# Attended rows stored from ScalarE's queue, four jobs later, in place of SyncE's queue

## The reference

```
z = rmsnorm(x) @ w_in                       # q, k, v and forget gate of group A; q, k, v of group B
A: softmax(q k' / 8 + C[t] - C[s]) v        # 8 heads of 64, causal, C = cumsum(log sigmoid(forget))
B: softmax(q k' / 8 + table[h, t - s]) v    # 8 heads of 64, own chunk of 64 and 8 chunks back
mix = concat(rmsnorm(A), rmsnorm(B)) @ w_out
x = x + rmsnorm(mix);  x = x + rmsnorm(swiglu(rmsnorm(x)))
```

## Time and profile before

| | |
|---|---|
| median of 3 runs | 3012.16 us (3006.19 to 3015.57) |
| profiled execution, its own time | 3007.07 us |
| its span, first to last instruction | 3005.3 us |
| PE busy, of the span | 2845.9 us, 95% |
| DVE, ACT, POOL busy | 57%, 38%, 25% |
| mean granted PE clock | 0.983 |
| `attend`, stretch 640 to 1290 | 650 us, 144 jobs |

### The profile page before, as it was taken

One profiled execution on the slowest core, in us unless ns is written; L12 is line 12 of the kernel. 1 busy time (PEld: TensorE's weight loads), 2 busy tenths in 40 slices (PEclk: granted clock), 3 DMA queues, 4 the chain that ended last, 5 costly groups with the idle time before them and its releaser, 6 DMA issues.

```text
span 3005.3 us, 54881 instructions
## 1 busy us (share of the span) xinstructions
PE 2845.9 (95%) x22143; PEld 2552.1 (85%) x22143; DVE 1709.5 (57%) x3122; ACT 1139.9 (38%) x1904; POOL 754.4 (25%) x683
## 2 busy tenths in 40 slices
PE   7999999979999789969989999999999999999998
PEld 7999999957777567758879999999999997887887
DVE  6222121168788577857788667776766662224443
ACT  5330000046666456645553334333433342223221
POOL 0000000054445123023345434544344420000000
PEclk9999999979999999989999999999999999999999
DMA  5322212152112897467733332332232345335553
GB/s 170 97 71 80 73 62 76 48 168 77 54 49 57 267 297 235 149 203 219 239 111 139 101 108 95 135 114 95 96 113 97 129 140 146 97 96 161 166 167 121
DMA packets 285539, 384.75 MB, mean 128 GB/s; under 512 B 24472, under 2 KB 211112, under 8 KB 273512
## 3 DMA queue, kind: packets, MB, share of 16 engines
q1 hardware_dynamic: 284984, 379.68, 40.0%
q10 hardware_dynamic: 304, 1.57, 0.2%
HBM read 291.91 MB, written 89.28 MB: 127 GB/s over the span
## 4 chain that ended last, share of the span: by engine, by line
PE 44%; issue 6%; DVE 3%; POOL 2%; DMA 1%; ACT 1%; SPq 0%; POOLq 0%; DVEq 0%; ACTq 0%
PE ffn_w L2174 3%; PE ffn_x L2174 3%; PE ffn_w L2177 3%; PE ffn_x L2177 3%; PE ffn_w L2176 3%; PE ffn_x L2176 3%; PE ffn_z L2177 3%; PE ffn_z L2174 3%; PE ffn_z L2176 3%; PE ffn_z L2208 1%; PE ffn_w L2208 1%; PE ffn_y L2174 1%; PE ffn_w L2210 1%; PE ffn_z L2210 1%; PE ffn_y L2177 1%
## 5 line engine op out<-in xcount | busy, mean ns | idle before, releaser
L1214 ACT ACTIVATE att_sx<-att_sx,att_nm 128x640 f32<-128x640 f32 (+17 forms) x272 | 263.4, 971 | 7.4 <-DVE att_nm L1348 7.4
L1225 ACT ACTIVATE att_pts<-att_pt 128x384 f32<-128x384 f32 (+3 forms) x296 | 145.3, 491 | 251.3 <-PE att_pt L1109 236.6
L80 PE MATMUL frt_pz<-frt_xhi,frt_hi 128*128 128x448 f32 (+1 forms) x640 | 230.5, 360 | 0.0
L82 PE MATMUL frt_pz<-frt_xhi,frt_lo 128*128 128x448 f32 (+1 forms) x640 | 230.5, 360 | 0.0
L81 PE MATMUL frt_pz<-frt_xlo,frt_hi 128*128 128x448 f32 (+1 forms) x640 | 230.0, 359 | 0.0
L1109 PEld LDWEIGHTS att_pt<-att_eye,att_sx 64*128 64x128 f32 x3296 | 129.9, 140 | 115.7 <-ACT att_pts L1225 60.1
L515 DVE TENSOR_TENSOR frt_shared<-frt_pz,frt_rb 128x448 f32<-128x448 f32 (+1 forms) x80 | 48.9, 612 | 313.5 <-PE frt_pz L82 313.5
L1109 PE MATMUL att_pt<-att_eye,att_sx 64*128 64x64 f32 x3296 | 166.5, 232 | 55.2 <-ACT att_pts L1225 18.3
L1147 PE MATMUL att_po<-att_pts,att_vv 128*64 128x128 f32 x3296 | 217.2, 279 | 0.3 <-issue 0.3
L1147 PEld LDWEIGHTS att_po<-att_pts,att_vv 128*64 128x64 f32 x3296 | 177.8, 137 | 45.1 <-ACT att_pts L1225 22.7
L1359 DVE COPY att_pts<-att_pt 128x384 f32<-128x384 f32 (+3 forms) x296 | 164.3, 555 | 64.6 <-PE att_pt L1109 58.4
(11 more groups left out here) (327 smaller groups left out, 8300.6 us busy)
## 6 DMA issues: line engine op xcount, KB each, us to landing
ahead_first<-mid_act SPq DMA_DIRECT2D x68, 704.0 KB, 6.7
ahead_second<-in_w_gu SPq DMA_DIRECT2D x33, 1024.0 KB, 5.4
ffn_wr<-in_w_gu SPq DMA_DIRECT2D x33, 1024.0 KB, 5.3
att_raw<-out_zT SPq DMA_DIRECT2D x64, 256.0 KB, 4.7
att_bb<-in_cache_ak SPq DMA_DIRECT2D x16, 1024.0 KB, 10.4
att_bb<-in_cache_av SPq DMA_DIRECT2D x16, 1024.0 KB, 8.3
mid_act<-ffn_ao SPq DMA_DIRECT2D x44, 362.0 KB, 2.5
out_zT<-frt_shared SPq DMA_DIRECT2D x64, 224.0 KB, 1.9
```

Source lines behind the costliest of these rows:

```text
L80: nc.tensor.matmul(out, a_hi(k), b_hi(k), start=(k == 0), stop=False)
L82: last = nc.tensor.matmul(out, a_lo(k), b_hi(k), start=False, stop=(k == kk - 1))
L1214: nc.scalar.activation(sx[n % NSX][:, e, :w], sx[n % NSX][:, e, :w], ACT.Exp, bias=nm[n % NSX][:, e:e + 1], scale=-1.0, accum_out=total).t ...
L1225: nc.scalar.activation(pts[G % NPT][:, :, 0:k, 64 * x:64 * x + 64], pt[x][:].rearrange("p (e j q) -> p e j q", e=2, q=64)[:, :, 0:k, :], A ...
```

## The change

`store` moves from SP's block to ACT's block without a change to what it transfers. SP no longer calls it. ACT calls `store(n - 4)` behind its work of the first turn of job n (behind the copy, and behind the exponentials where they stand there), and the last four at the end. `evict(n)` waits for `store(n - 4)` as before, so the store is now issued in the same job whose eviction needs its buffer. The wait in `store` is now ACT's.

```diff
             @block.sync
-                def store(n):
-                    kind, p, i = JOBS[n]
-                    evicted(sp, n)
...
-                    sp.dma_start(mixed(t)[i, :, p, :], os_[n % NOS][:]).then_inc(s_os[n % NOS], 16)
...
-                    if n >= 1:
-                        store(n - 1)
                     if kind != "stream" and p + 1 < NPAIR and 2 <= i < 10:
                         load_raw(8 * (p + 1) + i - 2)
-                store(NJOB - 1)
...
             @block.scalar
+                def store(n):
+                    kind, p, i = JOBS[n]
+                    evicted(act, n)
+                    if kind == "stream":
+                        band, b = divmod(p, NB)
+                        act.dma_start(mixed(t)[QB, :, band * CH:(band + 1) * CH, b * NQ:(b + 1) * NQ],
+                                     os_[n % NOS][:, 0:CH * NQ].rearrange("p (c t) -> p c t", c=CH)).then_inc(s_os[n % NOS], 16)
+                        return
+                    act.dma_start(mixed(t)[i, :, p, :], os_[n % NOS][:]).then_inc(s_os[n % NOS], 16)
...
                         if last_of(n, g):
                             for x in first_splits(n):
                                 split_high(x)
+                        if g == 0 and n >= 4:
+                            store(n - 4)
+                for n in range(NJOB - 4, NJOB):
+                    store(n)
```

## The result

The changed kernel takes 3059.10 us in the median (3054.88 to 3063.39), the kernel before 3012.82 in the same comparison (3006.19 to 3015.57), four runs each. The ratio is 1.0154, with a 95% interval of 1.0139 to 1.0170: 46 us slower. The forecast was 3002, and the range, 2995 to 3017, doesn't reach it. The profiled execution took 3063.39 us, with a span of 3061.7 and a mean granted clock of 0.976; it is 56 us above that of before (3007.07), so differences between the two profiles are some 10 us larger than between the medians.

The account below looks back on a forecast made before the run. PE was taken as the bound, with DMA nearly full from 1000 to 1120. Terms: 12.2 - 0 - 0.7 - 2 = 9.5 us off, 3007.07 to 2997.6; off the runs' median 3002.7, given as 3002, range 2995 to 3017.

Parts of the forecast that it names:

- part 6: Stores issued late on ACT's queue: landing under load taken as 4 us, bounds 1.6 and 7.7, adding 0.7 us of waits.
- The rival of late landing: Stores on ACT's queue land no sooner under load, so `evict` waits at most jobs: 20 us on, 3032; chance 0.12.
- Part 2: PE's lowered clock behind two of the three store waits no longer drops: 3 us off, bounds 0 and 3.
- the signs that the prediction named for being wrong: ACT issues over 1 us, PE's copy waits up over 2 us, store waits in pair-start jobs 17 to 20, new key waits.
- Part 1: Stores leave SP's load queue, so three waits at `evict` of jobs 71, 86 and 91 go: 7.2 us of PE off.
- part 5: 144 store issues added on ACT lie beside its exponentials: taken at 0, bounds 0 and 13 us.
- Part 7: From 1000 to 1120 the busy DMA engines take back some saved time: 2 us on, bounds 0 and 10.2.
- the rival of a DMA bound: DMA engines are the bound, so savings return as waits for keys and values: 3011, no gain; chance 0.14.
- Part 3: SP, not held by evictions, issues loads earlier, so PE's wait for stream 1's keys goes: 1.2 us off.
- Part 4: At the stage's end the reciprocals no longer stand behind SP's two stores: 0.8 us off, bounds 0 and 0.9.
- the rival of a held ACT: Issues hold ACT's engine or wait while SP's issue is stuck: 8 to 13 us, giving 3011 to 3016; chance 0.12.

## Why the prediction was wrong

**The step that failed is part 6**, which took 4 us for the landing under load and so 0.7 us for the waits. The landing measured 6.6 us in the median of 1010 to 1160 and up to 11.4, and 4.8 to 8.6 for the waited-for stores of the starts of the second and third fox pair. The intervals that the part worked out were about right (from a store's issue until its eviction is otherwise ready): 19 of 140 were under 5 us, where it had counted 25. The waits came to 62.0. The choice between the two ends was made by bytes: 6.3 us for 256 KB on ACT's queue, so less for 64. But a landing under load is in large part the wait behind what was issued before (5.5 of the 11.4 us of the store shown passed before its first packet), and the 32 KB of that store took 11.4 us where the 1 MB beside it took 15.3. The end of the range that I set aside, 7.7, was nearly the answer, and it had the right traffic in its row.

**The rival of late landing was the outcome**, with a chance of 0.12, above its deciding point of 6 us, and the range left it out. Its price of 20 us was also less than half of the 46. Two things were missing from it. The spread of landings costs more than a median of 7: a store of 11.4 makes a wait of 5.79. And the clock: behind the long stands PE ran at 0.50 to 0.82, and its busy time grew by 17.4 of the 54 us of the two profiles. Part 2 prices that effect for the three waits that go; the rival didn't price it for the waits that come. Counting half of the excess for overlap may have been too kind as well; no run separates that. Of the signs that the prediction named for being wrong, the waits at pair starts appeared (jobs 17 to 19, 34 and 35, 7.0 us), but they are a small part of the 62.0; 51.7 lie from 1010 on.

The Trainium skill ("DMA: Bandwidth & Descriptors", section "Issuing engines are not separate DMA queues") was the page that spoke against the change, and the trace and the run from GpSimd's queue (6.6 and 5.8 us in the median, from 7.7) agree with it. The Trainium skill's sentence on engines that go round between the queues (same page, section "Queues, rings and completion order") agrees with the second half of the case measured closely, the equal numbers of packets from 1048 to 1050 and the store that lands before an older load. It doesn't show in the first half: 5.5 us passed without a packet of ACT's queue beside hundreds of SP's. What the prediction drew from it, that a store on ACT's queue would not stand behind what SP has queued, failed by this delay ahead of the first packet.

**Part 1, the three waits go:** they didn't, other and more waits came. (Part 1 rests on the new path's leaving enough time; it names part 5 for this, but the term is in part 6.) That they can go, the kernel before with eight buffers from job 64 on shows, and also that PE stands as long elsewhere for it. **Part 2, the clock behind them:** right as a mechanism, 0.95 to 1.00 in 1030 to 1100 with eight buffers from job 64 on, and reversed in the changed kernel. **Part 7, what the DMA engines give back:** taken at 2 of 10.2, measured at about 8 by the same run. That run gained 2.2 us in its profile's second part and 4 in the medians, so even without a late store the forecast's 9.5 off was out of reach; the rival of a DMA bound was near the truth on this.

**Part 3, SP earlier:** not borne out. The wait for these keys stayed, 1.1 against 1.21 us. With late stores the free SP was a loss, since pacing it again gave 17 us back: a gain of 1.2 was booked. With stores three jobs later it cost nothing that can be seen. **Part 4, the end:** the reciprocals are issued 0.03 us behind the last eviction, and the next stage starts 3.36 us after it, before 3.76: 0.4, where 0.8 was booked.

```profile
1344.01 0.27 DVE L1379 COPY att_os<-att_po 128x128 f32<-128x128 f32 x1
1344.04 0.38 SPq L915 DMA_DIRECT2D mid_recips<-att_raw  x1
1344.12 0.41 ACTq L1209 DMA_DIRECT2D mid_mixT<-att_os  x1
1344.57 0.52 ACTq L1212 DMA_DIRECT2D mid_mixT<-att_os  x1
...
1347.37 1.14 ACTq L1643 DMA_DIRECT2D mix_rs<-mid_recips  x2
```

**Part 5, 144 issues at nothing:** right, from the earlier trace rows. ACT's timeline at a tight place of the changed kernel shows the issue beside the copy, and the two exponentials follow without a gap. The last three rows are for the other half of that rival, an issue of ACT's that waits while SP is stuck in one of its own: SP sits in a single issue of keys for 10.85 us, and ACT's two stores in that time take 0.33 us each.

```profile
732.93 0.49 ACT L1222 ACTIVATE att_pts<-att_pt 128x384 f32<-128x384 f32 x1 [0.50 <-PE att_pt L1096]
732.98 0.33 ACTq L1212 DMA_DIRECT2D mid_mixT<-att_os  x1
733.31 0.71 ACT L1201 ACTIVATE att_sx<-att_sx,att_nm 128x512 f32<-128x512 f32 x1
...
734.02 0.71 ACT L1201 ACTIVATE att_sx<-att_sx,att_nm 128x512 f32<-128x512 f32 x1
...
1016.23 10.85 SPq L839 DMA_DIRECT2D att_bb<-in_cache_ak  x1
...
1020.46 0.33 ACTq L1212 DMA_DIRECT2D mid_mixT<-att_os  x1
1023.94 0.33 ACTq L1212 DMA_DIRECT2D mid_mixT<-att_os  x1
```

The equal times with eight buffers say the same, and the rival of a held ACT falls, with both of its causes.

**What stays open.** What holds the first packet of a store back for some 4 us under load, when the engines then serve both queues side by side, no run tells. How SP's pace makes 17 us, by the spacing of its loads or by which stores the evictions then meet, is not separated. The fox part's own loss, some 9 to 14 us, was undone by lead and by buffers, and hardly by pace: the eviction of job 64 starts at 1019.8 in the changed kernel, at 1007.5 with stores three jobs later, at 1004.8 with eight buffers, at 1015.5 with SP paced, and at 1003.8 in the kernel before. Its traffic was not cut.

## What to carry to other kernels

Price a transfer that something waits for by two numbers: the interval from its issue to the need, and its landing in a stretch with the same traffic, whatever its own size and queue; take the landing's upper rows, since the longest ones make the waits. Moving the stores to a queue without loads bought 1.1 us of 7.7 here, and issuing them one job earlier or giving them more buffers bought back nearly all of the loss. When a long stand is added on the way to PE, add the clock behind it. And when stands are taken away in a stretch where the DMA engines are busy 0.9 of the time, look for how much of it can be kept: here it was the clock's share alone.

## What the runs showed of the hardware

- A 32 KB store on ACT's queue had no packet for 5.5 us beside 2.75 MB issued on SP's queue in the 6.4 us before it and with it, and landed in 11.4 us, where 1.6 is the least of that kernel's stores. From GpSimd's queue a 64 KB store took up to 9.2.
- Once its packets moved, the two queues' packets went side by side (356 and 358 in 2 us), and it landed 0.9 us before a load that SP had issued 1.1 us ahead of it. 25 of 35 stores on ACT's queue landed before an earlier load of SP's; on SP's own queue 0 of 48. The first packet of a store moved 3.6 to 4.1 us after the issue with three or more loads ahead (seven stores), 0.8 us with none (four).
- The landing follows the bytes ahead: 6.3 us in the median of 1010 to 1200, 2.6 with a quarter of the streams' cached keys and values.
- ACT's sequencer issues a store of 128 rows in 0.33 us beside queued activations, also while SP stood in one issue for 10.85 us. 169 us of such issues in place of 49, in a stage of 650, cost under 5.
- After a stand of 5.65 us PE ran the next 4 us at a granted clock of 0.50. Behind all eight evictions that waited over 3 us the clock of the next 4 us was 0.50 to 0.82; behind 16 of 23 shorter waits it was 1.00.
